# Gates of the first branch as two units of seven half-size products, in a fused three-branch block

## What is computed

```python
h = rms_norm(x, norm_g[l])
proj = h @ w_in[l]
...
y_a = ha * jax.nn.sigmoid(o_a) * jax.nn.silu(z_a)
...
g = jax.nn.sigmoid(gate.astype(jnp.float32)).astype(dt).reshape(B, S, N_BRANCH, D_MODEL)
merged = (g[:, :, 0] * (y_a @ w_branch[l, 0])
          + g[:, :, 1] * (y_b @ w_branch[l, 1])
          + g[:, :, 2] * (y_m @ w_branch[l, 2]))
x = x + merged @ w_out[l]
```

## Time and profile before

| | us |
|---|---|
| median of 3 runs | 960.03 (959.96 to 960.08) |
| the profiled execution | 960.33 |
| its span, first to last instruction | 958.5 |
| PE busy | 953.5 |
| DVE, ACT, POOL busy | 706.5, 534.8, 347.2 |
| four panels after the last head, with the numerators and turns | 825.6 to 917.3 |
| output product and last additions | 917.3 to 956.3 |

### The profile page before, as it was taken

The page is one execution under the profiler, slowest core; times in us unless marked ns, Lnnn a source line. Parts: engine busy times, 40 slices in busy tenths (PEclk is TensorE's granted clock), DMA queues, the critical chain, the costliest instruction groups (busy, mean ns, idle before and its releaser), DMA issues.

```text
span 958.5 us, 13405 instructions
## 1 busy us (share of the span) xinstructions
PE 953.5 (99%) x4897; PEld 839.7 (88%) x4897; DVE 706.5 (74%) x1079; ACT 534.8 (56%) x810; POOL 347.2 (36%) x247
## 2 busy tenths in 40 slices
PE   9999999999999999999999999999999999999998
PEld 7888888888989988988988888898998989988887
DVE  6879987688996676686688665895866958635586
ACT  6877644465456456546573422685765857732251
POOL 0100834456327137146120080462714527107500
PEclk9999999999999999999999999999999999999999
DMA  8624222144531531532355335616043150738312
GB/s 280 248 88 132 87 90 72 59 133 132 166 97 57 176 111 44 157 108 66 121 202 169 113 110 168 217 34 198 1 142 89 33 154 2 259 93 308 128 45 88
DMA packets 105157, 119.27 MB, mean 124 GB/s; under 512 B 4773, under 2 KB 80137, under 8 KB 104333
## 3 DMA queue, kind: packets, MB, share of 16 engines
q1 hardware_dynamic: 105084, 118.53, 38.5%
q10 hardware_dynamic: 16, 0.00, 0.0%
HBM read 106.45 MB, written 12.07 MB: 124 GB/s over the span
## 4 chain that ended last, share of the span: by engine, by line
PE 99%; DMA 1%; SPq 0%; ACT 0%; DVE 0%; issue 0%
PE proj L781 46%; PE proj L1141 12%; PE proj L1289 9%; PE att L1310 7%; PE proj L1310 5%; PE att L1360 3%; PE proj L951 2%; PE att L1105 2%; PE att L1123 2%; PE att L1048 1%; PE att L1070 1%; PE proj L1246 1%; PE att L1113 1%; PE att L1094 1%; DMA w_raw<-w_mem_kv_in 1%; PE att L1246 1%
## 5 line engine op out<-in xcount | busy, mean ns | idle before, releaser
L781 PE MATMUL proj<-hT_hi,w_hi 128*128 128x512 f32 x328 | 129.0, 393 | 0.0
L781 PE MATMUL proj<-hT_hi,w_lo 128*128 128x512 f32 x328 | 128.0, 390 | 0.0
L781 PE MATMUL proj<-hT_lo,w_hi 128*128 128x512 f32 x328 | 127.8, 390 | 0.0
L2131 DVE TENSOR_TENSOR w_lo<-w_raw,w_hi 128x2048 fp32r<-128x2048 f32 x28 | 68.2, 2434 | 53.2 <-ACT w_hi L1410 49.1
L1410 ACT ACTIVATE w_hi<-w_raw 128x2048 fp32r<-128x2048 f32 x28 | 53.6, 1915 | 72.1 <-PE proj L781 70.7
L781 PE MATMUL proj<-y_hi,w_hi 128*128 128x512 f32 x192 | 75.1, 391 | 0.0
L781 PE MATMUL proj<-y_hi,w_lo 128*128 128x512 f32 x192 | 74.8, 390 | 0.0
L781 PE MATMUL proj<-y_lo,w_hi 128*128 128x512 f32 x192 | 74.7, 389 | 0.0
L781 PEld LDWEIGHTS proj<-hT_hi,w_lo 128*128 128x128 f32 x328 | 61.6, 188 | 13.1
L781 PEld LDWEIGHTS proj<-hT_lo,w_hi 128*128 128x128 f32 x328 | 61.6, 188 | 12.3
L781 PEld LDWEIGHTS proj<-hT_hi,w_hi 128*128 128x128 f32 x328 | 61.6, 188 | 12.2
(11 more groups left out here) (522 smaller groups left out, 2923.8 us busy)
## 6 DMA issues: line engine op xcount, KB each, us to landing
w_raw<-w_in_in SPq DMA_DIRECT2D x36, 512.0 KB, 4.5
w_raw<-w_in_in SPq DMA_DIRECT2D x56, 256.0 KB, 3.8
w_raw<-w_branch_in SPq DMA_DIRECT2D x10, 1024.0 KB, 6.4
merged<-w_in_in SPq DMA_DIRECT2D x38, 256.0 KB, 3.6
merged<-w_in_in SPq DMA_DIRECT2D x14, 512.0 KB, 6.4
w_raw<-w_in_in SPq DMA_DIRECT2D x6, 1024.0 KB, 5.4
w_raw<-w_mem_kv_in SPq DMA_DIRECT2D x10, 512.0 KB, 6.7
yF<-x_in SPq DMA_DIRECT2D x8, 512.0 KB, 7.3
```

The lines of the kernel that those rows point to most:

```text
L781: ins = mm(ps, lhs[a](k, k0), rhs[b](k, k0), start=(first and k == 0 and j == 0), stop=(last and k == KH - 1 and j == 2))
L2131: V.tensor_tensor(w_lo[:, kh, :, 0:n], w_raw[:, kh, :, 0:n], w_hi[:, kh, :, 0:n].bitcast(F32), ALU.subtract).then_inc(w_lo_done, 1)
```

## The change

The gates of A are no longer two panels. They are two units of seven products; a product has 256 channels (two blocks `f`), half of the inner dimension and half of the tokens, 24 matmuls of 256 columns. Unit 0 makes channels 512 to 1023, unit 1 channels 0 to 511. Six operand slots are used instead of three (four quarters of `w_hi`/`w_lo`, the third slot, and `a_ath`/`a_atl` once the numerators are done). The eight sums of weight quarters run on VectorE. The numerators stand after product 1, the turns after product 4. After the 14 products come two whole panels of `y_a @ w_branch[0]`; the loops over mixed panels are gone. The loads follow: quarters of gate weights, then branch weights, `merged` and `w_out` later than before, and the second half of the last branch weights between two quarters of `w_out`.

```diff
-GA = _plan.take(4, 6, (4,) * 4)
+GA = _plan.take(2, 2, (2,) * 4)
+GATE_UNITS, GATE_SLOT = 2, (4, 0, 1, 2, 3, 4, 0, 5, 2, 3, 4, 5, 2, 4)
+GATE_RAW, GATE_SUM = "acaadbcaadabcc", {2: 1, 3: 3, 5: 2, 6: 4, 8: 5, 10: 7, 11: 6, 13: 8}
...
             sp.wait_ge(a_half, 2 * A_HEADS - 1)
+            for slot in "abdc":
+                gate_raw(1, slot)
+            sp.wait_ge(op_low, G_OP + PRODUCTS)
+            load(GA[0], [(wb[0], 0, 512)])
+            load_half(GA[0] + 1, wb[0], 512, 0)
+            sp.wait_ge(op_low, G_OP + 2 * PRODUCTS)
             sp.dma_start(merged[:, :], merged_kept).then_inc(kept_back, 16)
-            load(GA[0] + 1, [(wb[0], 0, 512)])
-            load(GA[0] + 2, [(wi, 512 + C_GATE, 256), (wb[0], 512, 256)])
             sp.wait_ge(a_y, 2 * A_HEADS)
+            sp.wait_ge(u_done, G_DONE + 2 * 12)
             for slot, dst, kh, c in (("d", out_b22, 1, 1), ("b", out_b12, 0, 1), ("a", out_b11, 0, 0), ("c", out_b21, 1, 0)):
+                if slot == "a":
+                    load_half(GA[0] + 1, wb[0], 512, 1)
+                    sp.wait_ge(u_done, G_DONE + 2 * 14)
...
-            gates_of(GA, {2: [lambda: a_numerators(g)], 5: [lambda: a_turn_h(g)]})
-            branch_of(GA, y_split(3))
-            with pe.Fori(2, 4) as j:
-                gated(GA, j)
+            def gate_product(n, rhs, to, start, before):
+                w = [op[GATE_SLOT[n]].rearrange("p (k n) -> p k n", k=KH) for op in (g_op_hi, g_op_lo)]
+                pe.wait_ge(op_low, G_OP + n + 1)
+                for f in range(2):
+                    pe.wait_ge(*before(f))
+                    for k in range(KH):
+                        for j, (a, b) in enumerate(((0, 0), (0, 1), (1, 0))):
+                            ins = mm(to[f][:, 0:HALF_T], w[a][:, k, f * P:(f + 1) * P], rhs[b](k), ...)
+                    ins.then_inc(u_done, 1)
...
+            gate_product(4, h_half_sum(3), second_pair, False, lambda f: (u_saved, G_SAVED + f + 3))
+            a_turn_h(g)
+            gate_product(5, h_half_sum(0), first_pair, False, lambda f: (u_saved, G_SAVED + f + 5))
+            gate_product(6, h_half(KH, HALF_T), first_pair, False, lambda f: (u_added, G_ADDED + f + 5))
+            gate_product(7, h_half(0, 0), last_pair, True, lambda f: (a_hnd, 4 * A_HEADS))
...
+            pe.wait_ge(u_added, G_ADDED + 12)
+            last_branch_panel(0, [(ys_lo, 3 * KT), None])
+            last_branch_panel(1, None)
... (VectorE)
+            def gate_low(n):
+                dve.wait_ge(op_high, G_OP + n + 1)
...
+            gate_low(3)
+            gate_low(4)
             a_denominators(g)
+            gate_low(5)
             a_variance(g)
+            gate_low(6)
             a_gated(g)
+            gate_low(7)
+            gate_sum(1, 1)
+            gate_add(4, mid, g_block(0, 1, 0), 6)
+            gate_sum(1, 2)
+            gate_low(8)
+            gate_add(5, low, g_block(0, 1, 1), 4)
+            gate_sum(1, 3)
... (ScalarE, behind the gates)
             act.wait_ge(t_done, A_TDONE + OUT_SUMS + 2)
             out_high(1)
-            gb_body(GA, 3, OUT[1] + 1)
+            split_hi(GA[0] + 1, 1, GA[1] + 2, 512, (3, GA[2][3] + 1))
+            split_hi(OUT[0], 0, OUT[1] + 1, 512)
```

More of the change, by code:

```diff
@@ L313, in hybrid_block @@
                                               enumerate(("out_b12", "out_b22", "out_b11", "out_b21")))
+        g_second = block_at("g_second", out_lo2_at)
+        g_of = [tabs[:, :, :, :].rearrange("p c t n -> p (c t n)").rearrange("p (b n) -> p b n", b=4),
+                g_second.rearrange("p (b n) -> p b n", b=4)]
+        g_raw = [dict(zip("abcd", [w[:, kh, c * D:(c + 1) * D] for kh in range(2) for c in range(2)]))
+                 for w in (w_flat[0], merged[:, :].rearrange("p (h n) -> p h n", h=2))]
+        g_op_hi = [w_flat[1][:, kh, c * D:(c + 1) * D] for kh in range(2) for c in range(2)] + [op_hi[2][:, 0:D], a_ath[:, 0:D]]
+        g_op_lo = [w_flat[2][:, kh, c * D:(c + 1) * D] for kh in range(2) for c in range(2)] + [op_lo[2][:, 0:D], a_atl[:, 0:D]]
         out_hi = [w_flat[1][:, 0], w_flat[1][:, 1], rounded("out_hi2", out_raw_at + 4 * KH * S * 2, KH * S)[:, :]]
@@ L439, in b_raw_of, with g_block, g_landed_of, g_free @@
             return b_w[B_RAW[n % B_OPS]][:, 0:width]
+        def g_block(u, f, h):
+            return g_of[u][:, 2 * f:2 * f + 2, h * HALF_T:(h + 1) * HALF_T]
+        def g_landed_of(u, slot):
+            if u:
+                return sig_landed["abcd".index(slot)], LAND0 + 16 * 5
+            return raw_landed[slot], G_RAW[slot] + 16
+        def g_free(n):
+            if n < 5:
+                return u_done, G_DONE - 2 * (2, 1, 1, 0, 0)[n]
+            if n == 7:
+                return a_num, 4 * A_HEADS
+            return u_done, G_DONE + 2 * max(m for m in range(n) if GATE_SLOT[m] == GATE_SLOT[n]) + 2
         def b_used(n):
@@ L734, in _, with gate_raw @@
             sp.wait_ge(op_low, A_OPLOW + last + 8)
[L735 to L738, removed]
+            def gate_raw(u, slot):
+                c0, kh = C_GATE + 512 * (1 - u) + 256 * (slot in "bd"), int(slot in "cd")
+                sp.dma_start(g_raw[u][slot].rearrange("p (k n) -> p k n", k=KH), w_cols(wi, kh * KH, c0, 256))\
+                    .then_inc(g_landed_of(u, slot)[0], 16)
+            gate_raw(0, "a")
+            gate_raw(0, "b")
+            sp.wait_ge(op_low, A_OPLOW + last + 10)
+            gate_raw(0, "c")
+            gate_raw(0, "d")
             sp.wait_ge(op_low, A_OPLOW + last + OPERANDS)
@@ L1345, in y_block, with last_branch_panel @@
+            gate_product(13, h_half(KH, HALF_T), last_pair, False, lambda f: (u_added, G_ADDED + f + 9))
+            def last_branch_panel(q, before):
+                panel(GA[0] + q, [(b, GA[2][b] + q, w_as_lhs(b * P), all_tokens(yT), S, before if b == 0 else None)
+                                  for b in range(4)])
+            pe.wait_ge(u_added, G_ADDED + 12)
+            last_branch_panel(0, [(ys_lo, 3 * KT), None])
+            last_branch_panel(1, None)
             def y_block(k0, t0):
@@ L1820, in _ @@
                 b_body(i)
[L1823 to L1834, removed]
             def ym_high(k):
@@ L2915, in _ @@
             second = merged_k[:, KH:KT, HALF_T:S]
+            dve.wait_ge(g_merged, 12)
             out_low_part(1)
-            gb_body(GA, 3, early_lows)
+            split_lo(GA[0] + 1, 1, 512)
+            split_lo(OUT[0], 0, 512)
+            early_lows()
+            for b in range(4):
+                gated_merge(1, b)
             merged_low(4)
```

220 lines of the change are left out of this document (148 added, 72 removed).

## The result

The changed kernel takes **964.9 us** (median of five executions, 963.9 to 968.2; their mean is 965.7), the kernel before 960.0; the ratio of the means is 1.006, 95% interval 1.004 to 1.008. The changed kernel is slower, by 4.9 us in the medians and 5.6 in the means, where 2.4 less were forecast, and outside the range. The profiled execution took 963.89, its span is 962.1 (before 958.5).

A forecast was written before the change was run, and what follows sets the result against it. TensorE's matmuls were taken to bound the kernel, busy 953.5 of 958.5 us. From the profiled 960.33, less 3.2 for matmuls, plus 0.8 for one wait, gave 957.9, a median of 957.6 us; range 956.5 to 959.5.

The forecast's parts named there:

- TensorE's own work: Gates: 192 matmuls of 512 columns (43.5 us) replaced by 336 of 256 columns at 0.120 (40.3 us), 3.2 us less.
- The Trainium skill's 4.7: Gates: saving by the skill's matmul gap formula, 41.4 - 36.7 = 4.7 us, set aside for the measured spacings.
- The wait at product 6: TensorE waits for VectorE's addition of product 5: 0.8 us, between nothing and 2.5; the one wait expected.
- my list of its steps: VectorE's queue from 821.99 to the denominators, summed to 13.5 us, arrival at 835.5.
- all other waits hold by 0.6 or more: Turns, product 4 and products 9 and 11: what they need is ready with at least 0.6 us to spare.
- The branch panels and output sums: After the products: ScalarE's queue, with `out_high(1)` behind two output sums, has the last panel's weights ready in time; no cost.
- Two us remain, so it costs nothing: Last branch panel: its weights ready by 902 at worst, needed at about 904.5.
- Their quarters of `w_out` are issued after product 11: Loads for two output sums on POOL: issued at about 865.7, landing at 877 to 880.
- the sum would not change: Last panel: if VectorE and GpSimd exclude each other, a low part takes 3.9 us, weights ready at 903.5, forecast time unchanged.
- The output product's first wait behind VectorE keeps about 1 us: Start of the output product: VectorE's work is ready with about 1 us to spare.
- Rival 4: Output quarters land late, ScalarE's queue delays the last panel's weights; costs from a landing 18 us after issue; chance 0.05.
- a restart of 0.2 to 0.4: TensorE after the wait at product 6: restarting adds 0.2 to 0.4 us, included in the 0.8.

The follow-up runs named there:

- e7: Changed kernel with all w_out quarters loaded early, and GpSimd's second half of the last head's gate made later, behind VectorE's low part of product 4: 958.8 us, ratio 0.9983.
- e1: Changed kernel with the 2 MB load of `merged` issued behind the first two quarters of `w_out` instead of ahead of them: 965.3 us.
- e2: Changed kernel with `merged` behind the first two quarters of `w_out` and the third quarter ahead of the last branch weights' second half: 960.6 us, ratio 1.0005.
- e3: Changed kernel with VectorE's low part of the output sum behind the four gated merges instead of ahead of them: 962.4 us, ratio 1.0025.
- e4: Changed kernel with VectorE's addition of product 5 ahead of a weight sum and the low part of operand 8: 963.9 us.
- c4: Kernel before, with unused VectorE subtractions of 128x2048 and 128x1024 ahead of its first output-product additions, so that TensorE waits 2.2 us: 963.98 us.

## Why the prediction was wrong

**TensorE's own work: right.** 336 matmuls of 256 columns at 0.120 (the chain pieces after 848.64: 2.88 for 24), 3.2 us less. The Trainium skill's 4.7 had no support before and gets none: with nearly all waits away the gain is 2.8.

**The wait at product 6: right in place, wrong in size.** 0.8 was the forecast, up to 2.5 its bound, 1.9 came. VectorE's arrival at the denominators was said as 835.5 and is 835.53; but everything began 0.85 earlier in this execution, so that VectorE took 0.9 longer than my list of its steps. That is the 0.9 by which the sum beside GpSimd's step is longer, and e7 takes it away. The normalised head then took 0.7 more than counted (7.24 against 6.5), because I had left GpSimd's second step at its 1.01 beside a low part of VectorE; it took 1.91. By this the turns waited 0.2 too, where I had written that all other waits hold by 0.6 or more. I had the place where the rule for this stands, and used it only for GpSimd's output sums: the Trainium skill (SBUF — State Buffer, "SBUF: two separate sides") says that a VectorE instruction with two SBUF operands and one of GpSimd shut each other out for their whole length. The rows agree to a tenth: GpSimd's step, asked for at 827.53, ends at 830.45, which is the end of VectorE's low part (829.31) and some 1.2 more, and VectorE's sum then ends at 831.54, 1.1 later. What the rows show beyond the rule: at 828.1, where one VectorE instruction ended and the next began, GpSimd did not get in. I should have looked for every GpSimd step in the stretch, not for the long ones.

**The branch panels and output sums: this step failed.** It ended with "Two us remain, so it costs nothing". Four things were wrong in it:

- I asked only when ScalarE's queue would be free of `out_high(1)`, which needs two of the four sums. That part held: `out_high(1)` began at 893.6. The other two sums and the subtraction `out_t` behind them were not followed to the low part that waits for them.
- "Their quarters of `w_out` are issued after product 11" is true of two. The third stands behind a weight half that waits for VectorE; it was issued at 873.8 and landed at 885.4, when the first sum had just ended. To move the others alone gives nothing (e1), to move all of them takes the wait away (e2).
- The twelve later sums were priced at 19.49, from a stretch where VectorE had little to do after 879 (one low part of 3.1 at 886.67). Moved to 885 to 910 they run beside merges and low parts, and take 25.0; VectorE's low parts of 2.29 grow to 3.2 and 3.4. The rule that I quoted says this, and I had written that by it "the sum would not change".
- "The output product's first wait behind VectorE keeps about 1 us" took the queue of before for the queue of after: four merges (some 6 us) now stand between the low part and the additions, where two stood, since the last panel is a whole one. e3 shows what the order is worth: 2.3.

No one of them alone explains it. With my own landing of 880 and my own price of the sums, 880 + 25.4 + 2.4 (`out_t` without VectorE beside it, as in e2) ends GpSimd at 907.8; `y_hi` and `y_lo` make 910.1, four merges 916.4 and the low part and two additions 918.2, against 920.9 when TensorE came. This margin of 2.7 was less than the 5.5 and 1.0 by which the twelve sums and `out_t` grew. That growth is read from the traces; no run changes it alone.

**Rival 4** named the right late loads and the right sign, but the wrong consumer, and gave it 0.05. Its threshold was about ScalarE, and the threshold of the real path was lower.

**The clock.** That a wait costs more than its length was in the text only as a restart of 0.2 to 0.4. The clock adds 1.3 to 1.6 in the profiles of most kernels, 2.7 to 2.8 in two, and nothing in some executions. Without it the changed kernel would be at 962.3, with two restarts at some 962.8: -3.2 + 1.9 + 3.6 is +2.3, still slower. The sign does not hang on the clock; some 2 of the 4.9 us in the medians do.

## What to carry over

Where a change moves loads or sums later, follow every result of the moved work to its last reader, one step past the first that proves harmless, and take the queue of the changed kernel, not of the old one, for what stands behind each wait. Price a GpSimd step by what VectorE does at the new time, and a VectorE step by what GpSimd does. Where TensorE comes to wait some two microseconds or more, as it did here, reckon with 1.3 to 2.8 more for the clock in some or all executions, and expect the time to scatter.

## What I had not expected of the hardware

- Behind waits of 2.2 to 5.6 us the profiles show TensorE at half rate (0.43 instead of 0.23), for 6 to 8 matmuls in four of them and for some 13 in two (e1, e4); the mean clock is 1.000 in all executions with a wait of 1.0 (10) and in all with 1.2 (9). Behind 1.9 (e2) and 2.2 (c4) some executions of the same kernel have 1.000 and others 0.998, and these take 1.6 and 1.3 us longer in the mean.
- Two short steps of GpSimd, 1.3 and 1.0 us long, took 2.9 and 1.9 beside VectorE and cost VectorE 0.9 of a 1.22 us sum. The first of them, moved 8 us, takes 1.3 and costs 0.2 (a low part of 1.43); the second, not moved, still takes 1.9.
- Twelve GpSimd sums took 19.5, 23.0, 24.4 and 25.0 us in four kernels with the same operands, as the load of VectorE beside them differed.
